# Depthwise convolution: the taps divided anew between TensorE, VectorE and GpSimd

## What is computed

```python
def conv_module(x, w_in, b_in, w_dw, b_dw, ln_g, ln_b, w_out, b_out):
    h = x @ w_in + b_in
    a, gate = jnp.split(h, 2, axis=-1)
    h = a * jax.nn.sigmoid(gate)
    h = lax.conv_general_dilated(
        h, w_dw[:, None, :], window_strides=(1,), padding=[(CONV_WIDTH - 1, 0)],
        dimension_numbers=('NWC', 'WIO', 'NWC'), feature_group_count=D_MODEL) + b_dw
    h = jax.nn.silu(layer_norm(h, ln_g, ln_b))
    return h @ w_out + b_out
```

## Time and profile before

| | us |
|---|---|
| median of 3 runs (1806.07 to 1806.15) | 1806.12 |
| the profiled execution, its time | 1807.27 |
| the same execution, its span | 1805.5 |
| TensorE busy | 1791.5 |
| VectorE busy | 1366.3 |
| ScalarE busy | 945.6 |
| GpSimd busy | 212.6 |

### The profile page before, as it was taken

How to read it: one execution, slowest core, us unless ns; L and a number is a source line. 1 busy time by engine, 2 the same in 40 slices (tenths; PEclk the granted TensorE clock), 3 DMA queues, 4 the chain that set the end, 5 groups by cost and what they waited for, 6 DMA issues and landing times.

```text
span 1805.5 us, 28004 instructions
## 1 busy us (share of the span) xinstructions
PE 1791.5 (99%) x10622; PEld 1570.1 (87%) x10622; DVE 1366.3 (76%) x2461; ACT 945.6 (52%) x1489; POOL 212.6 (12%) x122
## 2 busy tenths in 40 slices
PE   9999999999999999999999999999999999999998
PEld 9889998888888888888888899988888888888886
DVE  7975999888986665666666669998889866666665
ACT  5565445555555455555535454555555554555552
POOL 6720930000000000000004048000000000000000
PEclk9999999999999999999999999999999999999999
DMA  7544555555556566667733346555555566666772
GB/s 240 184 152 153 186 174 168 165 172 166 169 171 211 192 195 195 199 219 245 241 111 116 111 152 195 170 161 171 165 175 164 175 212 196 193 192 207 220 217 79
DMA packets 89413, 323.89 MB, mean 179 GB/s; under 512 B 10048, under 2 KB 10560, under 8 KB 89024
## 3 DMA queue, kind: packets, MB, share of 16 engines
q1 hardware_dynamic: 85248, 307.42, 53.3%
q10 hardware_dynamic: 4032, 14.68, 2.3%
HBM read 321.01 MB, written 1.05 MB: 178 GB/s over the span
## 4 chain that ended last, share of the span: by engine, by line
PE 89%; DVE 7%; DMA 1%; issue 1%; ACT 1%; POOL 0%; SPq 0%; DVEq 0%; ACTq 0%
PE y L662 40%; PE work L553 19%; PE work L556 10%; PE work L594 9%; PE y L934 3%; DVE y L1691 3%; PE work L612 2%; PE y L640 2%; PE work L615 1%; PE work L802 1%; PE y L907 1%; DMA raw<-conv_in 1%; DMA raw<-v 0%; DVE far_homes L483 0%; DMA raw<-u 0%
## 5 line engine op out<-in xcount | busy, mean ns | idle before, releaser
L483 DVE TENSOR_TENSOR low<-raw,high 128x1024 fp32r<-128x1024 f32 x385 | 470.6, 1224 | 136.8 <-ACT high L978 132.2
L978 ACT ACTIVATE high<-raw 128x1024 fp32r<-128x1024 f32 x431 | 453.5, 1053 | 198.3 <-PE work L556 97.6
L553 PE MATMUL work<-xT,high 128*128 128x512 f32 x1472 | 374.0, 396 | 0.1
L662 PE MATMUL y<-high,xT 128*128 128x512 f32 x1296 | 352.6, 390 | 0.0
L553 PEld LDWEIGHTS work<-xT,high 128*128 128x128 f32 x1472 | 264.1, 189 | 47.6 <-DVE low L483 0.5
L662 PE MATMUL y<-far_homes,xT 128*128 128x512 f32 x1320 | 304.8, 390 | 0.2 <-DVE xT L1603 0.2
L662 PEld LDWEIGHTS y<-far_homes,xT 128*128 128x128 f32 x1320 | 247.1, 188 | 51.7 <-DVE far_homes L483 0.6
L662 PEld LDWEIGHTS y<-high,xT 128*128 128x128 f32 x1296 | 243.0, 188 | 50.2
L1244 ACT ACTIVATE xT<-big 128x256 fp32r<-128x256 f32 x256 | 105.3, 416 | 256.8 <-PE y L662 251.4
L556 PEld LDWEIGHTS work<-xT,low 128*128 128x128 f32 x1472 | 200.8, 190 | 14.6
L556 PE MATMUL work<-xT,low 128*128 128x256 f32 x1472 | 205.0, 282 | 0.0
(11 more groups left out here) (208 smaller groups left out, 1818.8 us busy)
## 6 DMA issues: line engine op xcount, KB each, us to landing
raw<-u SPq DMA_DIRECT2D x256, 512.0 KB, 3.6
raw<-v SPq DMA_DIRECT2D x256, 512.0 KB, 4.3
raw<-wq SPq DMA_DIRECT2D x32, 512.0 KB, 3.7
raw<-conv_in SPq DMA_DIRECT2D x14, 512.0 KB, 4.4
aux<-ln_par ACTq DMA_DIRECT2D x9, 512.0 KB, 6.5
raw<-conv_out SPq DMA_DIRECT2D x8, 512.0 KB, 4.0
raw<-mla_out SPq DMA_DIRECT2D x8, 512.0 KB, 4.7
big<-diag ACTq DMA_DIRECT2D x6, 512.0 KB, 6.2
```

The lines of the kernel that those rows point to most:

```text
L483: ops.tensor_tensor(low_at(c), raw[:, slot, :], high_at(c).bitcast(F32), ALU.subtract).then_inc(low_made[slot], 1)
L553: nc.tensor.matmul(both, w_high[:, cols], xT[:, k], start=(k == 0), stop=False)
L662: mm = nc.tensor.matmul(y[:, 2 * h + m, :], a[:, a_slot, rows], v[:, m * 512:(m + 1) * 512], start=(start and n == 0), stop=(stop and n == 2))
L978: A(high_at(c), raw[:, slot, :], ACT.Copy).then_inc(high_made, 1)
```

## The change

TensorE's second chunk is now chunk 7, and it does only its taps 0 to 28. GpSimd, fed by ScalarE, adds taps 22 to 30 of chunk 4 first, then all of chunk 6, then taps 29 and 30 of chunk 7. VectorE's lanes do taps 0 to 16 and 17 to 21 of chunk 4; lane 1 begins tap 17 on top of GpSimd's sum. VectorE adds TensorE's total of chunk 7, the bias and GpSimd's two taps in a new instruction (`add_last`), ahead of the statistics of chunks 4 and 5; ScalarE's second copy falls away. ScalarE makes six products behind step 13 of the conv_in loop, two at step 14 and one at step 15; the high parts of blocks 17 and 18 move out of that loop, and with that of block 19 they stand behind products 12, 18 and 24 of 42 (`HIGHS_AT`).

```diff
--- before.py
+++ after.py
@@ -26,13 +26,19 @@
 PAD = TAPS - 1
 ROW = PAD + T + 2
 
-PE_CHUNKS = (5, 6)
-POOL_CHUNK = 7
+PE_CHUNKS = (5, 7)
+POOL_CHUNK = 6
 DIAG_LOADS = 4
 DIAG_AT = (4, 7, 10, 13)
-ROWS_AT, COPY_AT = 20, 20
+ROWS_AT, COPY_AT = 20, 29
 LANES = ((0, 1), (2, 3))
-SHARED, SHARED_TAPS = 4, 22
+SHARED, SHARED_TAPS, SHARED_END = 4, 17, 22
+LAST_END = 29
+POOL_TAPS = ([(SHARED, _w) for _w in range(SHARED_END, TAPS)] + [(POOL_CHUNK, _w) for _w in range(TAPS)]
+             + [(PE_CHUNKS[1], _w) for _w in range(LAST_END, TAPS)])
+FOR_SHARED = TAPS - SHARED_END
+PRODUCTS_AT = {13: 6, 14: 8, 15: 9}
+HIGHS_AT = (12, 18, 24)
 AHEAD = 12
 GLU_AT = {28: 2, 42: 3, 56: 4, 70: 5, 84: 6, 98: 7}
 PRODUCTS = 6
@@ -241,7 +247,7 @@
         row_stats = room(10, 64)
         diagonals = room(60, len(PE_CHUNKS) * TAPS * P).rearrange("p (c m) -> p c m", m=TAPS * P)
         products = room(0, PRODUCTS * T).rearrange("p (s t) -> p s t", t=T)
-        pool_sums = room(40, 2 * T).rearrange("p (s t) -> p s t", s=2)
+        pool_sums = room(40, 4 * T).rearrange("p (s t) -> p s t", s=4)
 
 
         keysT = room(73, 2 * NKEYS).rearrange("p (s n) -> p s n", s=2)
@@ -336,6 +342,7 @@
         product_ok = sem("tap_products_made")
         pool_step = sem("pool_step")
         pool_conv = sem("conv_on_pool")
+        pool_last = sem("last_taps_on_pool")
         pe_conv = sem("conv_on_tensor_engine")
         pe_conv_ok = sem("conv_on_tensor_engine_copied")
         rows_mm = sem("conv_rows_transposed")
@@ -504,14 +511,25 @@
                                     ALU.subtract).then_inc(low_made[0], 1)
             low_stage(3, FIRST["conv_out"] + 1)
 
-            for w in range(2, TAPS):
-                pool.wait_ge(product_ok, w + 1)
-                total, product = pool_sums[:, w % 2, :], products[:, w % PRODUCTS, :]
-                if w >= 4:
-                    pool.wait_ge(pool_step, w - 3)
-                nc.gpsimd.tensor_tensor(total, products[:, w - 2, :] if w < 4 else total, product,
-                                        ALU.add).then_inc(pool_step, 1)
-            pool.wait_ge(pool_step, TAPS - 2)
+            def tap_sums(first, taps, lane, done):
+
+                for w in range(2, taps):
+                    pool.wait_ge(product_ok, first + w + 1)
+                    total = pool_sums[:, lane + w % 2, :]
+                    if w >= 4:
+                        pool.wait_ge(pool_step, done + w - 3)
+                    nc.gpsimd.tensor_tensor(total, products[:, (first + w - 2) % PRODUCTS, :] if w < 4 else total,
+                                            products[:, (first + w) % PRODUCTS, :], ALU.add).then_inc(pool_step, 1)
+            tap_sums(0, FOR_SHARED, 2, 0)
+            pool.wait_ge(pool_step, FOR_SHARED - 2)
+            nc.gpsimd.tensor_tensor(pool_sums[:, 2, :], pool_sums[:, 2, :], pool_sums[:, 3, :],
+                                    ALU.add).then_inc(pool_step, 1)
+            tap_sums(FOR_SHARED, TAPS, 0, FOR_SHARED - 1)
+            last = FOR_SHARED + TAPS
+            pool.wait_ge(product_ok, last + 2)
+            nc.gpsimd.tensor_tensor(pool_sums[:, 3, :], products[:, last % PRODUCTS, :],
+                                    products[:, (last + 1) % PRODUCTS, :], ALU.add).then_inc(pool_last, 1)
+            pool.wait_ge(pool_step, FOR_SHARED - 1 + TAPS - 2)
             nc.gpsimd.tensor_tensor(conv[:, POOL_CHUNK, :], pool_sums[:, 0, :], pool_sums[:, 1, :],
                                     ALU.add).then_inc(pool_conv, 1)
             for c in OUT_LOWS_POOL:
@@ -735,9 +753,10 @@
             for c, k in enumerate(PE_CHUNKS):
                 pe.wait_ge(glu_ok, k + 1)
                 pe.wait_ge(diag_in[c], 16 * DIAG_LOADS)
-                for w in range(TAPS):
+                end = (TAPS, LAST_END)[c]
+                for w in range(end):
                     mm = nc.tensor.matmul(y[:, c, 0:T], diagonals[:, c, w * P:(w + 1) * P],
-                                          padded[:, k, w:w + T], start=(w == 0), stop=(w == TAPS - 1))
+                                          padded[:, k, w:w + T], start=(w == 0), stop=(w == end - 1))
                     if c == 1 and w == ROWS_AT:
                         pe.wait_ge(emptied, KD)
                         pe.wait_ge(glu_ok, KD)
@@ -752,7 +771,7 @@
             to_rows(SHARED).then_inc(rows_mm, 1)
             pe.wait_ge(pool_conv, 1)
             to_rows(POOL_CHUNK)
-            pe.wait_ge(pe_conv_ok, 2)
+            pe.wait_ge(conv_done, SHARED + 2)
             to_rows(PE_CHUNKS[1]).then_inc(rows_mm, 1)
             keep_clock(WARM_NORM)
 
@@ -1056,6 +1075,26 @@
                               diag[:, c, edges[0]:edges[1]]).then_inc(diag_in[c], 16)
 
 
+            made = [0]
+
+            def consumed(i):
+
+                first, done = (0, 0) if i < FOR_SHARED else (FOR_SHARED, FOR_SHARED - 1)
+                w = i - first
+                return done + (w + 1 if w < 2 else w - 1)
+
+            def products_to(n):
+                for i in range(made[0], n):
+                    made[0] += 1
+                    k, w = POOL_TAPS[i]
+                    if i in (0, FOR_SHARED, FOR_SHARED + TAPS):
+                        act.wait_ge(glu_ok, k + 1)
+                    if i >= PRODUCTS:
+                        act.wait_ge(pool_step, max(consumed(n) for n in range(i - PRODUCTS + 1)))
+                    bias = conv_p[:, C_BDW + k:C_BDW + k + 1] if w == 0 else 0.0
+                    A(products[:, i % PRODUCTS, :], padded[:, k, w:w + T], ACT.Identity,
+                      bias=bias, scale=tap(k, w)).then_inc(product_ok, 1)
+
             for t in range(2 * KD):
                 chunk, gate = divmod(t, 2)
 
@@ -1066,32 +1105,29 @@
                     bias = conv_p[:, C_BIN + KD + chunk:C_BIN + KD + chunk + 1]
                     A(value_gate[:, chunk, :], work[:, t % BANKS, 0:T], ACT.Sigmoid,
                       bias=bias).then_inc(emptied, 1)
-                make_high(t + RING)
+                if t < 2 * KD - 2:
+                    make_high(t + RING)
+                if t in PRODUCTS_AT:
+                    products_to(PRODUCTS_AT[t])
             for n in range(len(DIAG_AT), DIAG_LOADS * len(PE_CHUNKS)):
                 load_diagonals(n)
             for h in range(HALVES):
                 act.dma_start(x[:, h, :], x_rows[h]).then_inc(x_in, 16)
             ln_rows(0)
 
-            def copy_conv(c):
-                k = PE_CHUNKS[c]
-                act.wait_ge(pe_conv, c + 1)
-                A(conv[:, k, :], y[:, c, 0:T], ACT.Identity,
+            def copy_conv():
+                k = PE_CHUNKS[0]
+                act.wait_ge(pe_conv, 1)
+                A(conv[:, k, :], y[:, 0, 0:T], ACT.Identity,
                   bias=conv_p[:, C_BDW + k:C_BDW + k + 1]).then_inc(pe_conv_ok, 1)
 
-            act.wait_ge(glu_ok, POOL_CHUNK + 1)
-            for w in range(TAPS):
-                if w == 8:
+            for n in range(made[0] + 1, len(POOL_TAPS) + 1):
+                products_to(n)
+                if n in HIGHS_AT:
                     make_high(rounded[0])
-                if w == COPY_AT:
-                    copy_conv(0)
-                if w >= PRODUCTS:
-                    act.wait_ge(pool_step, 1 if w == PRODUCTS else max(2, w - PRODUCTS - 1))
-                bias = conv_p[:, C_BDW + POOL_CHUNK:C_BDW + POOL_CHUNK + 1] if w == 0 else 0.0
-                A(products[:, w % PRODUCTS, :], padded[:, POOL_CHUNK, w:w + T], ACT.Identity,
-                  bias=bias, scale=tap(POOL_CHUNK, w)).then_inc(product_ok, 1)
+                if n == COPY_AT:
+                    copy_conv()
             load_table(ACT.Sqrt, 0)
-            copy_conv(1)
             act.dma_start(keysT, keys[0]).then_inc(keys_in, 16)
             act.wait_ge(cvar_ok, 1)
             A(row_stats[:, 54:56], row_stats[:, 52:54], ACT.Sqrt).then_inc(cstd_ok, 1)
@@ -1685,6 +1721,7 @@
             def tap_sum(k, w, total, start, dst):
                 if start:
                     dve.wait_ge(glu_ok, k + 1)
+                if start and total is None:
                     bias = conv_p[:, C_BDW + k:C_BDW + k + 1] if w == 0 else None
                     return V.tensor_scalar(dst, padded[:, k, w:w + T], tap(k, w), bias, ALU.mult,
                                            ALU.add if w == 0 else ALU.bypass)
@@ -1700,7 +1737,7 @@
                 if n < len(LANES):
                     return LANES[n][lane], w, n
                 return SHARED, w + (0, SHARED_TAPS)[lane], n
-            lengths = (2 * TAPS + SHARED_TAPS, 2 * TAPS + TAPS - SHARED_TAPS)
+            lengths = (2 * TAPS + SHARED_TAPS, 2 * TAPS + SHARED_END - SHARED_TAPS)
             done = [0, 0]
 
             def next_tap(lane):
@@ -1709,13 +1746,20 @@
                     glu(GLU_AT[sum(done)])
                 k, w, n = chunk_of(lane, done[lane])
                 start = done[lane] % TAPS == 0
-                total = total_of(lane, n)
```

(19 more changed lines are left out.)

## The result

The changed kernel takes 1819.38 us (median of 4 runs, 1818.71 to 1820.55), the kernel before, on the same chip, 1806.13 (4 runs, 1806.07 to 1809.37). The ratio is 1.0071, its 95% interval 1.0057 to 1.0084: 13 us slower, where I forecast 1805.9. The profiled execution took 1820.55 us at a span of 1818.7, 13.2 more than the span before.

What follows compares the result with a forecast made beforehand. TensorE is busy 99% of the span, so only its waits and filler could be won. Of 1.25 us won before conv_out 0.2 remain, taken off the median of 1806.12: 1805.9 us, 8 of 10 within 1804.2 to 1807.3.

Steps and rivals of the forecast that it cites:

- Two SBUF inputs: VectorE's lane 1 tap 17, amid GpSimd's additions, reads both inputs from SBUF: 0.3 us lost, bounds 0 and 0.48.
- the granted clock: TensorE's wait from 84.1 to 85.75 leaves its clock at 1.00 (2.4 GHz): nothing put on it.
- The slower one: Rival: GpSimd is the last engine and holds the conv_out loads as well: 1806.5 to 1808 us, chance 0.21.
- The DMA issues do not hold the products back: Rival: ScalarE's chunk 6 products not held, or GpSimd otherwise 2 us earlier; TensorE's taps decide: 1804.1 us, chance 0.08.
- TensorE, two taps fewer: TensorE's conv taps: two fewer take 0.87 us off, so they end at 83.60.
- ScalarE: Chunk 6's first product starts only behind nine DMA issues, at 61.95 against 62.51: a gain of 0.56 us.
- GpSimd: Chunk 6's additions: the second stalls 0.66 us behind a rounding on ScalarE; the final addition ends at 85.40 without the lock.
- VectorE, fewer taps: VectorE's taps fall from 155 to 146: 3.74 us less, its last addition ending at 82.25.
- Behind the taps: From TensorE's transposes to conv_out: fillers decide, first conv_out product at 92.57 instead of 93.82, 1.25 us won.
- Where it is given back: In conv_out, later loads make TensorE wait for block 23's low part until 104.0: of 1.25 us, 0.2 remain.

Runs made afterwards that it cites:

- e1: The changed kernel with GpSimd's nine-tap sum copied by ScalarE into PSUM, where VectorE's tap 17 reads it: 1810.71 us, ratio 1.0021.
- e4: The changed kernel with GpSimd's addition of chunk 6's tap 24 waiting until VectorE's tap 17 is done: 1804.79 us, one execution.
- e5: The changed kernel with the nine-tap sum in PSUM and VectorE's addition of epsilon writing to PSUM: 1806.60 us, ratio 1.0000.
- f4: The changed kernel with 52 filler products more on TensorE behind its last tap: 1821.22 us, ratio 1.0075.
- f6: e1 with GpSimd's final addition of chunk 6 waiting for the one just before it: 1808.19 us, one execution.
- e2: The kernel before, with lane 1's first tap on chunk 4 (tap 22) given a tile of zeros in SBUF as second input: 1814.03 us, one execution.
- f7: e5 with block 23's low part on VectorE, and the x and layer norm DMA issues, three high parts and ScalarE's copy later: 1802.84 us, ratio 0.9977.
- e3: The changed kernel with GpSimd's addition of chunk 6's tap 24 waiting for the addition just before it: 1806.28 us, one execution.
- e9: The same edit of the changed kernel as e3, timed over 10 runs: 1807.34 us, ratio 1.0004.

## Why the prediction was wrong

**The step that failed** is "Two SBUF inputs". It named the instruction, its place "in the midst of GpSimd's additions" and that no row shows the pair, and then priced it at 0.3 us with bounds of 0 and 0.48. The term measured 14.48. The lower bound was sound; the upper one was not a bound. It took one instruction's length as the longest possible stall, because in the earlier trace rows the pass over x waited for one low part and got in ahead of the next. But that row was two low parts long, 93.39 to 99.14 in the trace of before, and stood right behind 1.74 us of idle time; it says nothing of an engine that has run without a pause for 13 us. The profile did show such a row: 29 additions 0.686 us apart, with low parts behind them. Had I asked for how long the other engine could hold on, the outer bound would have been GpSimd's next pause, near 92, some 14 us, and the range open upward. e1 to e4 show that this is what happens to the tap.

The same passage has a second gap: it looks at tap 17 alone and puts nothing on any other instruction. In the changed kernel the addition of epsilon came behind GpSimd's row (99.52, 0.17 us), because the tap had made it late; with the tap freed it was held for 4.97 us and cost 4.0 of the time (e1).

The Trainium skill (SBUF — State Buffer, Who interferes with whom) describes the lock as one held for an engine's whole instruction. By it the sum was 1806.1, 0.2 us nearer and just as wrong. These runs agree with it that the loser is shut out entirely (the tap ended 0.29 us behind GpSimd's last instruction) and that two SBUF inputs matter (14.96 against 0.48 us); they differ in that the tap was not let in between GpSimd's instructions while these followed without a pause.

**A term that was missing**: the granted clock. I wrote that a fall in the wait would make the prediction wrong, and priced it at nothing for a wait of 1.6 us; for 13 us the trace shows 2.18 us. The rows now at hand, TensorE's idle time ahead and what its 16 fillers then took: 1.57 and 3.74 (before), 1.96 and 3.74 (e5), 2.23 and 6.00 (f4), 2.55 and 5.36 (f6), 7.57 and 5.13 (e2), 13.0 and 5.92 (after). My wait of 1.65 us was rightly free; a longer wait costs, but not in proportion to its length.

**The rivals.** The slower one had the right sign and the wrong engine: it saw GpSimd late, not VectorE. None had a stall of VectorE beyond a microsecond. "The DMA issues do not hold the products back" was wrong for the kernel as it stood (4.34 us of issue ahead of 61.16); what I derived from it, that TensorE's taps then decide, is what f7 shows once they are moved.

**What held**, times of the changed kernel in its own trace, whose transposes are 0.75 us early. "TensorE, two taps fewer": end at 82.86, forecast 83.60 less 0.75. "ScalarE": chunk 6's first product at 61.16, forecast 61.95 less 0.75, right behind the last issue. "GpSimd": the stall after product 2 is 0.66 (63.98 less 62.63 less 0.69), forecast 0.66; the final addition ends at 84.57, forecast without the lock 85.40 less 0.75. "VectorE, fewer taps": the account above closes with 3.74 to 0.2 us. "Behind the taps" and "Where it is given back" could be tested only with the stall gone: e5's numbers are 1.43 won and 0.03 left, for 1.25 and 0.2. TensorE's wait there was 1.96 instead of 1.65 us. So with both held instructions out of the way the forecast of no change stands (e5, 1806.60); with only the tap out of the way it does not (e1, 1810.71).

## What to carry to other kernels

When an edit puts a VectorE instruction with both inputs in SBUF beside an unbroken row of GpSimd's SBUF instructions, its worst price is the time to GpSimd's next pause, not one instruction. The same held for one operation with a single SBUF input and an SBUF output (TENSOR_SCALAR), while a tap, the aggregate and the reciprocal with such operands passed. So look at every VectorE instruction beside the row, not only at the new one, and at how long the row is. A bound taken from a neighbouring row holds only if that row was in the same situation; where it was not, say so and leave the range open. And an instruction that stalls this way is counted as busy, so compare single durations of one shape, not busy shares or waits.

## What was not expected of the hardware

- VectorE's tap with two SBUF inputs: 1.17, 1.66 and 1.82 us with a pause close by (e4, e3, e9), 6.49 in e2, 14.96 in the changed kernel, 15.62 in f4; 0.48 with the second input in PSUM. Each time it ended at most 0.3 us behind GpSimd's pause; 0.08 us of pause was enough.
- A 2-column TENSOR_SCALAR from SBUF to SBUF is held as well: 4.97 us (e1), where 0.16 with its output in PSUM (e5). The 2-column aggregates (0.39 for two, e1) and reciprocal (0.17, e3), also from SBUF to SBUF, are not.
- GpSimd lost nothing by it in the changed kernel, its additions stood 0.69 us apart all the time; in before it lost 0.99 us to VectorE's pass, so the lock can fall to either.
- With a pause earlier in GpSimd's row the small addition got in at a border between two low parts (0.26 us in before, 0.38 in e3, 0.37 in f6), as the pass over x of the earlier trace rows did. What carries that over several microseconds is not settled.
